# First block of a two-block model: recurrence, attentions and branches placed between the weight pages, with small inverses and norms on rows

## What is computed

```python
h = rms_norm(x, norm1_g)
p_rwkv, p_sb, q_mem, gate_logits = split(h @ w_in)            # 1792, 1536, 512, 3072 columns
y_a = rwkv7_branch(p_rwkv, ...)                                # 8 heads of 64
y_b = stick_breaking_branch(p_sb, ...)                         # 8 heads of 64, scores, log-sums, weights
y_m = memory_branch(q_mem, mem, ...)                           # kv = rms_norm(mem) @ w_mem_kv, softmax, 4 heads of 128
merged = sum over n of sigmoid(gate_logits[n]) * (ys[n] @ w_branch[n])
x = x + merged @ w_out
x = x + conv_ffn(x)                                            # up, causal convolution, silu gate, down

def rwkv7_branch(p):
    p = p + (previous token of p - p) * mu                     # token shift
    r, k, v, wl, al, gl = split(p)
    decay, a = from w0 + tanh(wl) @ w2, sigmoid(a0 + al @ a2)
    g  = sigmoid(gl) @ g2
    kk = k * k_k, divided by its norm over each head
    # per token: S = S * decay - (S kk) (kk * a) + v k;  y = S r
    y  = (normalised over each head) * lnx_g + lnx_b + bonus
    return y * g
```

## Time and profile before

| | |
|---|---|
| median of the runs | 1602.0 us |
| the profiled execution | 1604.44 us, its span 1602.6 us |
| mean granted TensorE clock | 0.951 |
| PE busy | 1367.9 us, 85% |
| DVE | 917.9 us, 57% |
| ACT | 623.3 us, 39% |
| POOL | 545.1 us, 34% |
| DMA | 381.03 MB, 238 GB/s over the span |

### The profile page before, as it was taken

How to read it: one execution, slowest core, us unless ns; L and a number is a source line. 1 busy time by engine, 2 the same in 40 slices (tenths; PEclk the granted TensorE clock), 3 DMA queues, 4 the chain that set the end, 5 groups by cost and what they waited for, 6 DMA issues and landing times.

```text
span 1602.6 us, 19190 instructions
## 1 busy us (share of the span) xinstructions
PE 1367.9 (85%) x7122; PEld 976.8 (61%) x7122; DVE 917.9 (57%) x1853; ACT 623.3 (39%) x1427; POOL 545.1 (34%) x370
## 2 busy tenths in 40 slices
PE   6988968985977799999999989999878777878776
PEld 5877857954867799999978864444322222322222
DVE  2222896605252667743672567667667667666644
ACT  2002312214242466655544535444444444444433
POOL 0000000000026578887401534444443434434441
PEclk9998978967999899999999999999999999999999
DMA  5443310001324445565423489999999999999995
GB/s 203 147 142 93 118 53 1 1 0 53 106 79 145 132 156 185 176 196 170 132 81 120 170 327 421 421 421 421 421 421 421 422 408 413 408 421 422 422 421 238
DMA packets 67641, 381.03 MB, mean 238 GB/s; under 512 B 7520, under 2 KB 7648, under 8 KB 34400
## 3 DMA queue, kind: packets, MB, share of 16 engines
q0 software_dynamic: 36864, 268.45, 40.4%
q1 hardware_dynamic: 29808, 107.49, 20.7%
q10 hardware_dynamic: 880, 3.93, 0.7%
HBM read 378.79 MB, written 1.05 MB: 237 GB/s over the span
## 4 chain that ended last, share of the span: by engine, by line
PE 52%; DMA 28%; DVE 12%; ACT 5%; issue 2%; POOL 1%; DVEq 0%; SPq 0%; ACTq 0%; POOLq 0%
DMA arena_block<-in_experts,arena_block 27%; PE bank L397 24%; PE bank L847 6%; PE bank L413 4%; PE bank L425 2%; DVE arena_mix L1343 2%; PE bank L802 2%; DVE late L1832 2%; PE bank L529 1%; PE bank L537 1%; PE bank L669 1%; PE bank L535 1%; PE bank L395 1%; PE bank L436 1%; DMA ring<-in_pages 1%
## 5 line engine op out<-in xcount | busy, mean ns | idle before, releaser
L847 PE MATMUL bank<-arena_block 128*128 128x512 f32 x1024 | 500.6, 624 | 117.3 <-ACT arena_block L1237 117.1
L1877 POOL TENSOR_TENSOR w_lo<-ring,w_hi 128x1024 fp32r<-128x1024 f32 x110 | 269.5, 2465 | 644.2 <-ACT w_hi L905 644.1
L847 PEld LDWEIGHTS bank<-arena_block 128*128 128x128 f32 x1024 | 184.2, 194 | 423.6 <-ACT arena_block L1237 267.8
L1832 DVE SCALAR_TENSOR_TENSOR late<-arena_block 128x1024 f32<-128x1024 f32 x256 | 313.3, 1225 | 208.0 <-DMA arena_block<-in_experts,arena_block 168.0
L1887 POOL DMA_INDIRECT arena_block<-in_experts,arena_block x256 | 275.5, 1076 | 387.5 <-PE bank L847 353.5
L1231 ACT ACTIVATE arena_block<-arena_block 128x1 f32<-128x1 f32 x256 | 51.8, 202 | 350.8 <-DVE late L1832 349.9
L905 ACT ACTIVATE w_hi<-ring 128x1024 fp32r<-128x1024 f32 x110 | 115.5, 1053 | 100.0 <-PE bank L425 36.7
L397 PE MATMUL bank<-h_norm,ring 128*128 128x256 f32 x576 | 130.2, 385 | 3.0 <-ACT arena_mix L918 3.0
L397 PEld LDWEIGHTS bank<-h_norm,ring 128*128 128x128 f32 x576 | 109.6, 192 | 20.9 <-issue 6.1
L397 PE MATMUL bank<-arena_mix,ring 128*128 128x256 f32 x480 | 106.1, 384 | 14.5 <-DMA ring<-in_pages 14.5
L397 PE MATMUL bank<-x_hi,w_hi 128*128 128x256 f32 x416 | 118.3, 284 | 0.0
(11 more groups left out here) (399 smaller groups left out, 2152.3 us busy)
## 6 DMA issues: line engine op xcount, KB each, us to landing
ring<-in_pages SPq DMA_DIRECT2D x192, 512.0 KB, 3.5
late<-in_pages SPq DMA_DIRECT2D x8, 512.0 KB, 9.0
arena_block<-in_experts,arena_block POOLq DMA_INDIRECT x256, 15.3
const<-in_const ACTq DMA_DIRECT2D x1, 1136.0 KB, 9.3
x_res<-in_xT SPq DMA_DIRECT2D x2, 512.0 KB, 7.3
arena_mix<-in_memT ACTq DMA_DIRECT2D x1, 1024.0 KB, 13.0
arena_block<-in_subkT ACTq DMA_DIRECT2D x1, 1024.0 KB, 4.9
out_tok<-arena_block SPq DMA_DIRECT2D x4, 256.0 KB, 4.8
```

The lines of the kernel that those rows point to most:

```text
L847: last = mm(bank[2 * tt + j][:, :], diag[:, slot, :], uv[slot][:, D + j * 512:D + (j + 1) * 512], start=False, stop=stop)
L1832: stt(junk[r % 2], uv[s][:, 0:D], 1.0, htok[:, tt, :], ALU.mult, ALU.mult, accum_out=e_act[:, s:s + 1])\
L1877: nc.gpsimd.tensor_tensor(w_lo[:, slot, :], ring[:, slot, :], w_hi[:, slot, :].bitcast(F32), ALU.subtract)\
```

## The change

The first block is written anew as one stream of pages with everything else between them, in three chains: recurrence, attentions, branches.

- The pages of `in_a` come in the order `A_ORDER` (low-rank tiles, k, r, v, then the attentions'). Each tile is evicted and shifted by itself (`evict`).
- Head norms: the sums land on 8 or 12 rows (`C_PAIR`, `C_HOT`), root and reciprocal run on `row`, 8 or 12 x 256, and a matmul with `C_SPREAD` spreads them. Those of the attention's k and of the memory's q are taken by token (`col`) and go in as a scale at the read of the scores.
- The inverses keep the four 32x32 blocks on the diagonal of each item as 32 columns (`DTn`, `DDn`, `PPn`, `Cn`), and make them in four levels of 32x32 matmuls (`near_product`); steps to 64 and to 128 follow (`pp32` to `dd64`). The masks `C_LEVEL` are gone. `near_pp` and `near_dd` alternate with pages and with the groups of pair scores (`pairs`).
- A branch page holds two output tiles of four blocks each, is multiplied as plain float32, and its result is multiplied by its gate at the read of the bank (`branch` on VectorE). The order is gate0, br0, gate1, gate2, br2, br1. `out` is plain too: `SPLIT0` is now `up`.
- The barriers are gone; each engine has one counting semaphore for this block (`b_pe`, `b_act`, `b_dve`), with the steps numbered in `B_PE`, `B_ACT` and `B_DVE`.
- At the end of the kernel `y_square(0)` is two calls, inside group `PH` of the rows, and `y_root(0)` stands inside the next group.

```diff
-STAGES = ["in_a", "sbv", "mk", "mv", "gate", "branch", "out", "up", "down", "in2", "tv", "qk", "ti", "g2", "out2", "wq"]
-COUNTS = [N_IN_A, N_SBV, N_MK, N_MV, N_GATE, N_BR, N_OUT, N_UP, N_DOWN, N_IN2, N_TV, N_QK, N_TI, N_G2, N_OUT2, N_WQ]
+STAGES = ["in_a", "sbv", "mk", "mv", "gate0", "br0", "gate1", "gate2", "br2", "br1", "out", "up", "down", "in2", "tv", "qk", "ti", "g2", "out2", "wq"]
+COUNTS = [N_IN_A, N_SBV, N_MK, N_MV, 8, 4, 8, 8, 4, 4, N_OUT, N_UP, N_DOWN, N_IN2, N_TV, N_QK, N_TI, N_G2, N_OUT2, N_WQ]
...
-SPLIT0 = PAGE0["branch"]
+SPLIT0 = PAGE0["up"]
...
+A_ORDER = [12, 13] + list(range(4, 8)) + list(range(0, 4)) + list(range(8, 12)) + list(range(14, 26))
...
+    c[0:64, C_PAIR + 6] = 1
+    c[64:P, C_PAIR + 7] = 1
+    for ft in range(4):
+        c[:, C_SPREAD + P * ft:C_SPREAD + P * (ft + 1)] = p == 2 * ft + f // 64
+    c[:, C_MEAN] = np.where(np.arange(P) < 8, 1.0 / SHD, 1.0 / MHD)
...
-    def barrier(eng, k):
-
-        eng.drain().then_inc(S("phase_done"), 1)
-        eng.wait_ge(S("phase_done"), 3 * k)
```

The work on TensorE between pages, the small products and the pairs:

```diff
-        def wide(page0, n, hi, lo=None):
-
-            for k in range(n):
-                page_ready(page0 + k)
-                ways = products(page0 + k, hi, lo)
-                for j in range(KT):
-                    for n_, (w, y) in enumerate(ways):
-                        last = mm(bank[j][:, 0:T], w[:, j * P:(j + 1) * P], y[:, k, :], start=k == 0 and n_ == 0,
-                                  stop=k == n - 1 and n_ == len(ways) - 1)
+        def branch(stage, n):
+
+            for b in range(4):
+                page = PAGE0[stage] + b
+                page_ready(page)
+                for t in range(2):
+                    bank_free(pe, TILE0[stage] + 2 * b + t)
+                    for k in range(4):
+                        last = mm(bank_of(stage, 2 * b + t)[:, 0:T], ring[:, page % SLOTS, t * 512 + k * P:t * 512 + (k + 1) * P],
+                                  ys[:, 4 * n + k, :], start=k == 0, stop=k == 3)
...
+        def near_product(out, left, right):
+            for j in range(ITEMS):
+                for b in range(0, P, NEAR):
+                    r = slice(b, b + NEAR)
+                    last = mm(bank[out][r, j * NEAR:(j + 1) * NEAR], left[r, j, :], right[r, j, :], start=True, stop=True)
+            return last
+
+        def near_pp(lv):
+            pe.wait_ge(S("b_dve"), B_DVE[f"inv{lv - 1}"] if lv else B_DVE["near_ready"])
+            pe.wait_ge(S("b_act"), B_ACT["bktok_taken"])
+            near_product(6, Cn, DDn).then_inc(S("b_pe"), 1)
+
+        def near_dd(lv):
+            pe.wait_ge(S("b_act"), B_ACT[f"pp{lv}"])
+            near_product(7, DTn, PPn)
+            near_product(6, PPn, DTn).then_inc(S("b_pe"), 1)
...
+            for hh in range(4):
+                _, ft, o = item(0, 4 * (G % 2) + hh)
+                c = G // 2
+                last = mm(bank[4 + hh % 2][:, (hh // 2) * T:(hh // 2 + 1) * T], (kT if side else bT)[o:o + 64, ft, c * P:(c + 1) * P],
+                          AR[o:o + 64, ft, c, :, :], start=True, stop=True)
```

The list of TensorE from the second page on, and the loop over the levels:

```diff
+        pe.wait_ge(S("b_act"), B_ACT["lora_taken"])
+        up4(lambda ft: lora_w[:, 1, ft * P:(ft + 1) * P], lambda ft: proj[:, 13, :], P).then_inc(S("b_pe"), 1)
+        a_page(6, 2)
+        pe.wait_ge(S("b_dve"), B_DVE["kk_sq"])
...
+        a_page(8, 2)
+        pe.wait_ge(S("b_dve"), B_DVE["kk_inv"])
+        for ft in range(4):
+            last = mm(bank[6 + ft // 2][:, (ft % 2) * T:(ft % 2) * T + T], cst(C_SPREAD + P * ft)[0:8, :], row[0:8, :], start=True, stop=True)
+        last.then_inc(S("b_pe"), 1)
+        a_page(10)
+        pe.wait_ge(S("b_act"), B_ACT["gate_taken"])
...
+        for lv in range(4):
+            a_page(18 + 2 * lv)
+            near_pp(lv)
+            pairs(2 * lv)
+            a_page(19 + 2 * lv)
+            near_dd(lv)
+            pairs(2 * lv + 1)
```

VectorE's eviction, its part of a level and of a branch:

```diff
+        def evict(b, shift=False):
+
+            i = A_ORDER[b]
+            dve.wait_ge(S("page_done"), PAGE0["in_a"] + b + 1)
+            tt_(proj[:, i, :], bank_of("in_a", b)[:, 0:T], norm_at[0][2], ALU.mult).then_inc(S("in_a_out"), 1)
+            if shift:
+                d = shd[:, b % 4, :]
+                dve.wait_ge(S("in_a_out"), b + 1)
+                tt_(d[:, 1:T], proj[:, i, 0:T - 1], proj[:, i, 1:T], ALU.subtract)
+                step(ts(d[:, 0:1], proj[:, i, 0:1], -1.0, None, ALU.mult))
+                return stt(proj[:, i, :], d, V("mu", i), proj[:, i, :], ALU.mult, ALU.add)
...
+        def near_cross(lv):
+            dve.wait_ge(S("b_pe"), B_PE[f"pp{lv - 1}"])
+            tt_(Cn, Mn, level(lv + 2), ALU.mult)
+
+        def near_add(lv):
+            dve.wait_ge(S("b_pe"), B_PE[f"dd{lv}"])
+            tt_(DDn, DDn, two(bank[7][:, :], NEAR), ALU.add)
+            tt_(DTn, DTn, two(bank[6][:, :], NEAR), ALU.add).then_inc(S("b_dve"), 1)
+
+        def pairs_read(j):
+            side, G = j // 4, j % 4
+            dve.wait_ge(S("b_pe"), B_PE[f"pairs{j}"])
+            for q in range(2):
+                pb = bank[4 + q][:, :].rearrange("p (h s t) -> p h s t", h=2, s=2)
+                hs = slice(4 * G + q, 4 * G + 4, 2)
+                if side == 0:
+                    ts(MT[:, hs, :], pb[:, :, 0, :], -1.0, None, ALU.mult)
+                    last = tt_(RB[:, hs, :], pb[:, :, 1, :], incl, ALU.mult)
+                else:
+                    tt_(KA[:, hs, :], pb[:, :, 0, :], strict, ALU.mult)
+                    last = tt_(RK[:, hs, :], pb[:, :, 1, :], incl, ALU.mult)
+            last.then_inc(S("b_dve"), 1)
...
+        def branch(stage, n, b):
+
+            dve.wait_ge(S("page_done"), PAGE0[stage] + b + 1)
+            dve.wait_ge(S("gate_out"), 8 * n + 8)
+            for j in (2 * b, 2 * b + 1):
+                gj = gates[:, 8 * n + j, :]
+                if n == 0:
+                    tt_(merged[:, j, :], bank_of(stage, j)[:, 0:T], gj, ALU.mult).then_inc(S("branch_out"), 1)
+                else:
+                    tt_(gj, bank_of(stage, j)[:, 0:T], gj, ALU.mult).then_inc(S("branch_out"), 1)
+            if n:
+                dve.wait_ge(S("branch_out"), OUT_SEM[stage][1] + 2 * b + 2)
+                for j in (2 * b, 2 * b + 1):
+                    last = tt_(merged[:, j, :], merged[:, j, :], gates[:, 8 * n + j, :], ALU.add)
+                    if n == 1:
+                        last.then_inc(S("merged_in"), 1)
```

ScalarE at the end of the kernel:

```diff
+                if j == PH and r in (4, 8):
+                    y_square(0, r // 4 - 1)
+                if j == PH + 1 and r == 4:
+                    y_root(0)
...
-            if j == PH:
-                y_square(0)
-            if j == PH + 1:
-                y_root(0)
-        y_square(1)
+        y_square(1, 0)
+        y_square(1, 1)
         y_root(1)
```

More of the change, by code:

```diff
@@ L443, in token_scale, with a_page, item @@
             last.then_inc(S("rtok_up"), 1)
[L445 to L451 removed]
+        def a_page(first, n=1):
+            linear("in_a", xg, part=(first, n))
+        def item(c, h):
+            return 8 * c + h, h // 2, (h % 2) * 64
@@ new lines, in _ @@
+        last.then_inc(S("b_pe"), 1)
+        linear("gate2", hn, part=(2, 2))
+        pe.wait_ge(S("b_act"), B_ACT["mem_flip"])
+        for h in range(MH):
+            for mt in range(2):
+                last = mm(bank[4 + h][:, 0:T], mv[:, h, mt, :], att_t[h][:, mt, :], start=mt == 0, stop=mt == 1)
+        last.then_inc(S("b_pe"), 1)
+        linear("gate2", hn, part=(4, 4))
+        pe.wait_ge(S("b_act"), B_ACT["mem_out"])
+        branch("br2", 2)
+        branch("br1", 1)
+        linear("out", merged, ready=("merged_in", 0))
@@ new lines, in _ @@
+        last.then_inc(S("b_act"), 1)
+        for lv in range(4):
+            act.wait_ge(S("b_pe"), B_PE[f"pp{lv}"])
+            A_(PPn, two(bank[6][:, :], NEAR), ACT.Copy).then_inc(S("b_act"), 1)
+        act.wait_ge(S("b_dve"), B_DVE["inv3"])
+        for b in range(0, P, NEAR):
+            r = slice(b, b + NEAR)
+            last = A_(DT[r, :, r], DTn[r, :, :], ACT.Copy)
+        last.then_inc(S("b_act"), 1)
+        take("sbv", flat(sbv), part=(0, 1))
+        act.wait_ge(S("b_pe"), B_PE["pp32"])
@@ new lines, in _ @@
+        for a in range(NEAR, P, 64):
+            r = slice(a, a + NEAR)
+            last = A_(PPn[r, :, :], two(bank[6][r, :], NEAR), ACT.Copy)
+        last.then_inc(S("b_act"), 1)
+        take("sbv", flat(sbv), part=(1, 1))
+        act.wait_ge(S("b_pe"), B_PE["dd32"])
+        for a in range(0, P, 64):
+            r = slice(a, a + NEAR)
+            last = A_(DT[r, :, a + NEAR:a + 64], two(bank[6][r, :], NEAR), ACT.Copy)
+        last.then_inc(S("b_act"), 1)
+        take("sbv", flat(sbv), part=(2, 1))
@@ L1024, in _ @@
-        att_exp("mem", 0)
-        take("gate", gates, ACT.Sigmoid, part=(20, 4))
-        for h in range(MH):
-            if h + 1 < MH:
-                att_exp("mem", h + 1)
-            att_take("mem", MHD, ys[:, 8:12, :], h)
-        barrier(act, 3)
-        for page in range(SPLIT0, SPLIT0 + 3):
-            high(page)
```

(30 more changed lines are left out.)

1025 lines of the change are left out of this document (532 added, 493 removed).

## The result

The changed kernel takes 1506.23 us (median of four runs, 1501.86 to 1511.92), the kernel before 1600.95 in the same comparison: ratio 0.9409, interval 0.9371 to 0.9448. The forecast was 1478 with a range of 1461 to 1526: the time lies inside, 28 us above the forecast. The gain is 95 us where 124 were worked out for the first block.

The account below looks back on a forecast made before the run. TensorE's list was taken to bound the first block: 413.9 + 8.5 + 7 + 3 + 4 = 436.4 us against 560.2. Then 1604.4 - 123.8 - 2 = 1478.6, median 1476, stated as 1478; range 1461 to 1526.

Parts of the forecast that it names:

- Work of TensorE: First block up to the first `up` page: pages and small matmuls at full clock, start included, sum to 413.9 us.
- mode changes: First block: a page after narrow matmuls takes 0.2 us more; some 35 such places, 7 us.
- Waits on other engines: First block: TensorE waits for the kk reciprocal 5, branch 0's bank about 2, attention weights 1.2, lora 0.3; together 8.5 us.
- level units: Inverses in the first block: two pages, 192 small matmuls and two pair groups take TensorE 13.3 us, VectorE about 6.
- one long wait and two short ones: 3: First block: pages run slower after TensorE idles, 1.9 us after a long wait; 3 us in all.
- rival C: The first block's interleaved part settles at clock 0.50 and costs double: 377 us more, 1855; chance 4%.
- Tight hand-overs: First block: each costs between nothing and 0.78 us; ten at 0.4 make 4 us.
- The end: End of the kernel: cutting the half-way norm in two and moving its root gains between 0 and 3.4, taken as 2 us.
- main case: Whole kernel: the forecast together with D, 1464 to 1497 us, chance 60%.
- A: First block's 32-wide matmuls cost 58 ns, not 22: 57 us instead of 21, time 1513; chance 13%.
- B: First block: long hand-overs between pages, each bringing slow clock, 11 x 4.1 = 45 us, time 1523; chance 16%.
- D: First block: plain branches and `out` cost 11.5 us more work, returning waits another 12: 1490; 60% with the forecast.

Follow-up runs that it names:

- e_wide2: The changed kernel with each group of 64 small matmuls in the levels replaced by one matmul of 128 rows by 512 columns: 1487.08 us.
- e_double: The changed kernel with the product of each level that feeds the copy made twice, 256 small matmuls more in all: 1530.16 us.
- e_tail: The kernel before with only the changed end, the half-way square in two calls and its root inside the next group: 1602.23 us.

## Why the prediction was right, and where it was 28 us off

The mechanism was right: TensorE's list sets the first block, the block's earlier end passes one for one to the end of the kernel, and the gather has its 660 us. Term by term up to the first `up` page, forecast 436.4, measured 461.0:

- Work of TensorE. Forecast: 413.9, less the 14.5 start, the 2.0 of the slow first page and the 1.4 of waiting in the 4.9, plus 7 for mode changes, is 403.0. Measured: 461.0 less the start 12.8, the 1.6 of the slow first page (5.10), the pauses 15.7, slow clock 18.6 (22.2 less 2.6 behind 461 and 1.0 while TensorE stood still anyway) and the waits 10.4, is 401.9. Pages, small matmuls, the 11.5 us for plain branches and `out`, and the 0.2 us behind narrow ones (pages of 3.65 us) are within it; singly some may be off and cancel.
- Waits on other engines: 8.5 + 1.4 forecast, 10.4 measured.
- The step that failed is the one on level units. "A level unit takes TensorE 13.3 us" holds only for a TensorE that has its instructions. Its four pauses and that of the first group cost 15.7 us: e_wide2 takes the levels' pauses away, e_double makes eight of the four. The sum had no term for them. The price per matmul was taken from 32 in a row between pages, too few to empty a block; I had summed durations and never counted instructions.
- The clock: "one long wait and two short ones: 3" was mis-sized; it was 22.2, in eight stretches. 11.9 of it stand behind the pauses or the wait for the reciprocal. The two with TensorE busy could have been read from the 0.50 at 340 us, which I gave to rival C only as a whole.
- Tight hand-overs, 4 us: not there beyond the waits above. TensorE began 1.7 us earlier, which is not the change's doing: e_tail, the kernel before but for its end, began at 13.2. These two make up for part of the miss by luck.
- The end, 2 us: nothing (e_tail).

24.6 us were missing at the first `up` page (pauses 15.7, clock 15.6, waits 0.5, less 1.7 and 0.4 at the start, 4 of hand-overs and 1.1 of work), 2.7 behind it in its norm sum at slow clock (6.10 instead of 3.45), and 3.4 at the end, the 2 us and 1.4 more of the other sign; 30.7 on the profiled execution, 28 in the medians.

That the time lies in the range is in part luck. The main case, 1464 to 1497, does not hold 1506; the range reached further for the sake of A and B, and neither came.

Rival A named a unit of 17 us as its sign, and the units did take 16 to 18. The sign was badly chosen: it could not part dearer matmuls from a pause between them. The rule of the Trainium skill, TensorE: Matmul & The Clock Gate, section "Wait — 56ns, not 53.3ns?", that starts never come closer than about 25 ns, does not hold here: 128 records in 1.29 us. The 1506 that the prediction worked out by it equals the measured time by chance. B and C did not come; D's 11.5 us came, its 12 us of waits did not.

Open: why some blocks take 4.0 and others 4.7 us beyond what the packets' own times tell; whether three pages to a level, which would give each block more work, ends the pauses (not tried); and what starts the slow stretches at 228 and 265 us.
